# Expert front: weight splits ahead of the first gathered part, last gather behind the first unit

## What is computed

```python
def hierarchical_moe(h, ...):
    grp_w, grp_idx = lax.top_k(softmax(hf @ w_router_grp + b_router_grp), 1)
    ...
    top_logit, top_idx = lax.top_k(sel_logits, TOP_K_IN_GROUP)
    ...
    for g in range(N_GROUPS):
        a = jnp.einsum('nd,edf->nef', hf, w_gate[g])
        u = jnp.einsum('nd,edf->nef', hf, w_up[g])
        y = y + jnp.einsum('nef,efd->nd', jax.nn.silu(a) * u * comb[:, g, :, None], w_down[g])
```

## Time and profile before

| What | Value |
|---|---|
| median of 3 runs | 3108.92 us (3106.68 to 3109.06) |
| the profiled execution | 3108.28 us |
| its span | 3106.5 us |
| PE busy | 98% |
| DVE, ACT busy | 66%, 46% |
| mean granted PE clock | 0.994 of full speed |

### The profile page before, as it was taken

One profiled execution on the slowest core, in us unless ns is written; L12 is line 12 of the kernel. 1 busy time (PEld: TensorE's weight loads), 2 busy tenths in 40 slices (PEclk: granted clock), 3 DMA queues, 4 the chain that ended last, 5 costly groups with the idle time before them and its releaser, 6 DMA issues.

```text
span 3106.5 us, 46886 instructions
## 1 busy us (share of the span) xinstructions
PE 3057.5 (98%) x15988; PEld 2555.1 (82%) x15988; DVE 2044.6 (66%) x4032; ACT 1421.2 (46%) x2280; POOL 168.8 (5%) x305
## 2 busy tenths in 40 slices
PE   7999999999999999999999999999999999999999
PEld 6698876868887688899888888888989988888887
DVE  6567752546774351998777777765289976677776
ACT  2436642335663243156354444444315634444444
POOL 3110000200000000410000000000032000000000
PEclk9989999999999999999999999999999999999999
DMA  8758897745889633433655555553243255565554
GB/s 330 252 185 313 301 351 271 281 131 192 310 307 350 235 108 96 137 102 102 197 186 189 192 189 189 189 182 135 90 137 108 93 193 191 190 192 190 189 189 149
DMA packets 167141, 614.73 MB, mean 198 GB/s; under 512 B 18752, under 2 KB 18784, under 8 KB 166096
## 3 DMA queue, kind: packets, MB, share of 16 engines
q1 hardware_dynamic: 151632, 551.62, 52.2%
q0 software_dynamic: 15360, 61.16, 5.2%
HBM read 611.66 MB, written 1.05 MB: 197 GB/s over the span
## 4 chain that ended last, share of the span: by engine, by line
PE 94%; DVE 3%; DMA 1%; ACT 1%; issue 0%; DVEq 0%; POOL 0%; ACTq 0%; SPq 0%; POOLq 0%
PE PS L1656 13%; PE PS L1657 13%; PE PS L1658 13%; PE PS L2307 11%; PE PS L1702 7%; PE PS L2267 6%; PE PS L2309 6%; PE PS L2188 4%; PE PS L2290 4%; PE PS L1716 2%; PE PS L1743 2%; PE PS L1977 2%; PE PS L2173 2%; PE PS L2026 1%; PE PS L2299 1%; PE PS L2135 1%
## 5 line engine op out<-in xcount | busy, mean ns | idle before, releaser
L1028 DVE TENSOR_TENSOR w_lo<-arena,w_hi 128x1024 fp32r<-128x1024 f32 x448 | 529.9, 1219 | 0.0
L627 ACT ACTIVATE w_hi<-arena 128x1024 fp32r<-128x1024 f32 x448 | 451.5, 1048 | 103.2 <-DMA arena<-in_v_t 77.2
L1656 PE MATMUL PS<-w_hi,pw_hi 128*128 128x512 f32 x1024 | 401.4, 392 | 2.8 <-DVE w_lo L1028 2.3
L1657 PE MATMUL PS<-w_lo,pw_hi 128*128 128x512 f32 x1024 | 400.7, 391 | 0.0
L1658 PE MATMUL PS<-w_hi,pw_lo 128*128 128x512 f32 x1024 | 398.4, 389 | 0.0
L2307 PE MATMUL PS<-x_lh,w_hi 128*128 128x512 f32 x1536 | 379.4, 389 | 0.0
L2307 PEld LDWEIGHTS PS<-x_lh,w_hi 128*128 128x128 f32 x1536 | 288.2, 188 | 59.7
L973 ACT ACTIVATE arena<-PS 128x256 f32<-128x256 f32 x192 | 73.9, 385 | 444.1 <-PE PS L2309 444.1
L1251 DVE TENSOR_TENSOR gu_lo<-raw,gu_hi 128x1024 fp32r<-128x1024 f32 x192 | 222.7, 1220 | 16.9 <-ACT gu_hi L719 16.7
L1658 PEld LDWEIGHTS PS<-w_hi,pw_lo 128*128 128x128 f32 x1024 | 192.3, 188 | 41.5
L1656 PEld LDWEIGHTS PS<-w_hi,pw_hi 128*128 128x128 f32 x1024 | 193.0, 188 | 39.1 <-issue 2.6
(11 more groups left out here) (420 smaller groups left out, 5220.7 us busy)
## 6 DMA issues: line engine op xcount, KB each, us to landing
arena<-in_u_t SPq DMA_DIRECT2D x256, 512.0 KB, 4.5
arena<-in_v_t SPq DMA_DIRECT2D x256, 512.0 KB, 3.6
raw<-in_w_gu SPq DMA_DIRECT2D x192, 512.0 KB, 5.3
arena<-in_w SPq DMA_DIRECT2D x152, 512.0 KB, 3.6
arena<-in_w_ada POOLq DMA_DIRECT2D x96, 512.0 KB, 7.0
raw<-in_w_down SPq DMA_DIRECT2D x96, 512.0 KB, 5.5
arena<-in_w_gu SPq DMA_DIRECT2D x64, 512.0 KB, 7.0
arena<-in_w_down SPq DMA_DIRECT2D x32, 512.0 KB, 4.9
```

Source lines behind the costliest of these rows:

```text
L627: A(w_hi[:, m % RING], ring[:, m % RING], ACT.Copy).then_inc(S["hi_done"], 1)
L1028: V.tensor_tensor(w_lo[:, m % RING], ring[:, m % RING], w_hi[:, m % RING].bitcast(F32), ALU.subtract)\
L1656: mm(dst, w[0], m[0], start=start, stop=False, skip_group_check=skip)
L1657: mm(dst, w[0], m[1], start=False, stop=False, skip_group_check=skip)
```

## The change

Three moves, the same for both layers. On ACT and on DVE, part 0 is handled behind the splits of m0 to m3 and no longer ahead of them. On PE, `gather(3)` with its wait stands behind the up matmuls of unit 0 and no longer ahead of them. No instruction is added or removed, and no transfer is changed.

```diff
@@ ACT, moe(l)
-                gathered(0)
                 weights_hi(0, 0)
                 weights_hi(0, 1)
+                gathered(0)
                 act.wait_ge(S["rt_dve"], 7 * l + RT_DVE["top"])
@@ PE, moe(l)
                 gather(2)
-                pe.wait_ge(S["ga_lo"], GA_N * l + 1)
-                gather(3)
                 u0 = NU * l
@@ PE, loop over units
                     if u == 0:
+                        pe.wait_ge(S["ga_lo"], GA_N * l + 1)
+                        gather(3)
                         pe.wait_ge(S["ga_lo"], GA_N * l + 3)
```

## The result

| | before | after |
|---|---|---|
| median of 8 runs each | 3108.03 us (3105.26 to 3109.06) | 3118.31 us (3114.80 to 3120.27) |
| profiled execution | 3108.28 us | 3119.32 us |
| its span | 3106.5 us | 3117.5 us |

The ratio is 1.0032, with a 95% interval of 1.0024 to 1.0041: slower by 10.3 us in the medians and 11.0 us between the two spans. The forecast was +8.0 us, and its value of 3116.6 stands 1.7 us under the median.

What follows compares the result with a forecast made beforehand. PE, busy 98% of the span, was taken as the bound. Waits of 5.42 us plus 3.2 for the clock less 0.58 for a weight slot gave +8.0 us: 3116.6 us, range 3112.4 to 3119.5.

Steps and rivals of the forecast that it cites:

- No gain on PE: PE from gather(3) and unit 0 to the shares: gather(3) takes 1.38 us in either place, shares stay at 225.53, gain 0.
- The wait ahead of unit 2: PE's wait for hht_lo grows to about 3.35 us in layer 1; cost 2.81 and 2.61 us, together 5.42.
- The clock: PE's granted clock falls to about half behind the wait ahead of unit 2: 1.6 us a layer, 3.2 us for both.
- The one wait for a down slot, -0.58: PE's one wait for a weight slot, 0.58 us at 274.42, should go: -0.58, between -0.58 and 0.
- Rival 1: Waits ahead of unit 2 come, clock does not fall in both layers: 3113.1 to 3113.7, or 3114.7 to 3115.3; chance 0.30.
- Rival 2: m15 late for unit 3, or clock low for a second 3.2 us: adds 0.3 to 1.6 us a layer; chance 0.10.
- Rival 3: Not slower: unit 0's earlier start carries through to hht_lo and waits vanish, -1.8 us, 3106.5 to 3107.1; chance 0.05.
- Rival 4: Nothing happens: the 4.1 us by which unit 0's Silu is late is absorbed, 3108 to 3110; chance 0.05.

Runs made afterwards that it cites:

- e2: Kernel before with only the PE move (gather(3) behind unit 0), ACT and DVE as before; +10.5 us, ratio 1.0033.
- e3: The whole change, with part 3 also moved behind unit 0's Silu on ACT and its hidden values on DVE; -0.4 us against the kernel before, ratio 0.9998.
- e5: The whole change, with m4 and m5 handled ahead of part 3 on ACT and DVE; +2.1 us against the kernel before, ratio 1.0005.
- e8: The whole change, with part 3 moved behind the Silu of unit 0 on ACT alone; +7.3 us against the kernel before, ratio 1.0023.
- e6: The whole change, with 13 small constant matmuls on PE behind the transposes of sel; +4.7 us against the kernel before, ratio 1.0016.
- e4: The whole change, with 16 small constant matmuls on PE behind unit 2's wait for m9; +12.7 us against the kernel before, ratio 1.0039.
- e1: Kernel before with only the ACT and DVE moves (part 0 behind m0 to m3), gather(3) still ahead of unit 0; +7.1 us, ratio 1.0022.

## Why the prediction was right, point by point

**No gain on PE.** Right: the argument was that PE had no wait between `gather(2)` and the shares, so there was nothing to win; the shares moved by 0.25 us. In the profile of the change PE had no wait ahead of unit 0, and e2 shows that the ACT and DVE moves are what keeps it away (1.1 us).

**The wait ahead of unit 2.** Right in mechanism, place and size. Predicted unit 2 at 236.75, measured 236.94; cost 2.81 and 2.61 predicted, 2.75 and 2.65 measured (3.29 less 0.54 and 0.64). ACT's wait for `gather(3)` was 5.6 us where about 4 was foretold, which costs nothing by itself: what counts is when the wait ends. (The prediction counts 16 matmuls in each gather; the traces have 8, 32 for all four. The 1.38 us for one are right.) e3 removes the cause and the wait goes; e5 and e8 remove parts of it and the wait shrinks by what the working of each said.

**The clock.** Right, and it was the choice between two ends far apart: 3.2 us for two slow stretches, or 0. By the first row of unit 2 and of the transposes behind it, its up matmuls took 7.17 us (236.94 to 244.11) in the changed kernel and 5.55 before (233.94 to 239.49), 1.6 us a layer as taken. In e6, with the wait filled, the clock stayed full. That each slow stretch cost 1.6 us and not more is partly luck: behind the same wait e2 lost 2.8 and 2.6. The trace of the kernel before held a second case, among light matmuls, that the prediction passed over: in its second router PE waited 1.88 us until 724.24, and from 725.6 to 728.8 the clock was 0.50. The rule of the Trainium skill that was weighed for this ("TensorE: Matmul & The Clock Gate", Part 1: half speed is where the array falls when idle) pointed the same way, and the stretches of the change and of e6 agree with it. As it was put, with no length of the wait, it would have had the clock fall behind e5's 1.4 us too, where it stayed at 1.00.

**The one wait for a down slot, -0.58.** Wrong, and the one step that failed. It was "should go"; the changed kernel waits 0.55 us in the first layer (at 279.07) and 0.90 us in the second (at 908.16), where before there had been one of 0.58. The total of PE's waits for `dn_lo` from 228 to 1080 us:

```profile
PE PS L1656 <- DVE dn_lo L1251: 1.4, 2, 0.9
```

So the term is +0.9 and not -0.58. The argument that slots would shift by less than PE was right for m12 to m15 (no wait ahead of unit 3), but I carried it on to slots 30 us later, at which I had not looked. All the other kernels but e8 also have waits of 0.5 to 1.0 us for `dn_lo` in one layer or both, so they come and go with small shifts and are hardly an effect of the change.

**The 1.6 us in between.** Not in the prediction. In the changed kernel's second router the clock fell within a run of light matmuls, with PE hardly waiting:

```profile
722.00:725.00 3.00, 2.81 (x26) 2.58 (x25) 2.73 (x10) 2.61 (x6) 0.00 (x0) 1.00 0.00 0
725.60:728.60 3.00, 3.00 (x18) 2.81 (x17) 0.12 (x2) 0.85 (x2) 0.00 (x0) 0.53 0.03 5
```

The kernel before lost the clock within these matmuls (L1904 and L1900) in the first layer, from 199.8 us on, and not in the second, where it fell only at 725.5; the changed one the other way round. The row of the kernel before, over the same matmuls of its second layer:

```profile
717.00:724.00 7.00, 5.18 (x47) 4.75 (x45) 3.88 (x20) 5.56 (x10) 0.00 (x0) 1.00 0.01 2
```

That stretch is the same code in both kernels, so I take it for scatter between executions. It was argued, not tested. The forecast of 8.0 so lies 2.3 us under the measured 10.3: its terms for the waits and the clock, 8.6 together, came to 8.6 in the trace (2.75, 2.65, 1.6 and 1.6); the slot missed by 1.5, and the scatter of the routers was in no term.

**Rivals.** Rival 1 (no fall of the clock in both layers) is refuted for waits of 2.5 us (e4, e8) and 3.3 us and holds for one of 1.4. Rival 2 (m15 late, or a second slow stretch) did not occur in the profile of the change; e2 shows 5 us at 0.50 behind the same wait, so the longer slow stretch is real. (Its range, 3117.5 to 3119.8, was added to two different bases; from 3116.6 it is 3117.2 to 3119.8.) Rival 3 (a gain carried through) is what e3 sets up, and it gives -0.4 us with the waits still at 0.6. I had put up to 1.8 us on it. Rival 4 is refuted by the wait itself.

## What to carry to other kernels

When a step moves later on one engine, read the queues of the engines that consume its result: the cost is not the step, it is what stands behind its consumer in an in-order queue, here 2.1 us of splits and a table load of 1.3 on ACT, and 2.3 us of splits on DVE. If the consumers are moved with it (e3) the move is free; if only one of two is (e8), most of the cost stays. And count a new wait on PE at more than its length once the traces show the clock falling behind waits of that size: here a wait that grew by 2.7 us cost 4.3. When effects are as small as here, compare one stretch of the two timelines before the totals: what lay outside it, the clock in the routers above all, moved the spans of single executions by up to 3 us.

## What the runs showed of the hardware

- The clock behind a wait in dense matmuls: after 1.39 and 1.40 us (e5) it stayed full; after 2.05 us it fell and after 2.36 us it did not (e1, two layers of one execution); after 2.46 and 2.47 us (e4), 2.53 and 2.52 us (e8) it fell, and with all four waits of 3.29 us (the change, e2), in e2 already within the wait. In e8 the 3.0 us from 237.0 had 0.54 of the clock and those from 759.5 had 0.50. So a wait between 2 and 2.4 us may go either way.
- The slow stretch is no fixed price: about 1.6 us of lost time in the change, but over 5 us at 0.50 and 2.8 and 2.6 us of lost time in e2 with a wait of the same length.
- Light matmuls without a wait can lose the clock too (rows 722 to 728.6 above).
- Some small DVE instructions took two to four times as long when they fell into POOL's subtractions (L556). In the changed kernel a part of `sel` that takes 0.42 us took 0.95, and the cast of L1186 took 0.73 us inside POOL's first run (205.61 to 207.71) where the kernel before, just behind that run, took 0.17. Rows of DVE's timeline and of POOL's:

```profile
210.04 0.42 DVE L1210 TENSOR_TENSOR sel<-cst,arena 128x256 fp32r<-128x256 f32 x1
210.58 0.95 DVE L1210 TENSOR_TENSOR sel<-cst,arena 128x256 fp32r<-128x256 f32 x1
```

```profile
210.48 3.76 POOL L556 TENSOR_TENSOR hg_lo<-h,hg_hi 128x256 fp32r<-128x256 f32 x5 [2.77 <-PE PS L1675]
```

  It is the same instruction on the other half of the tokens, and POOL starts at 210.48, between the two. No run here took POOL's work away, so that POOL is the cause was not tried.
